# Turning the operands of a router's products, with a copy and a transpose to turn the logits back

## The reference

```
gp = softmax(ht @ rg_w + rg_b)                  # 4 groups
g_idx = argmax(gp); g_prob = gp[g_idx]
el = (ht @ re_w + re_b).reshape(T, 4, 8)[g_idx]  # 8 experts of the chosen group
top_p, top_i = top_k(softmax(el), 2)
gates = g_prob * top_p / sum(top_p)
# each token then goes through its 2 experts, of 32:
y = (silu(x @ w_gate[e]) * (x @ w_up[e])) @ w_down[e]
```

## Time and profile before

| | us |
|---|---|
| median of 3 runs | 1764.89 |
| the runs | 1764.3, 1764.89, 1767.46 |
| the profiled execution, its own time | 1770.13 |
| its span | 1768.2 |
| TensorE busy | 1724.3 (98%) |
| VectorE busy | 863.0 (49%) |
| mean granted clock of TensorE, of full | 0.993 |

### The profile page before, as it was taken

The page is one execution under the profiler, slowest core; times in us unless marked ns, Lnnn a source line. Parts: engine busy times, 40 slices in busy tenths (PEclk is TensorE's granted clock), DMA queues, the critical chain, the costliest instruction groups (busy, mean ns, idle before and its releaser), DMA issues.

```text
span 1768.2 us, 23681 instructions
## 1 busy us (share of the span) xinstructions
PE 1724.3 (98%) x9694; PEld 1136.4 (64%) x9694; DVE 863.0 (49%) x1522; ACT 485.0 (27%) x742; POOL 23.5 (1%) x31
## 2 busy tenths in 40 slices
PE   7999999999999999999999999999999999999997
PEld 6879999987789999844444444347674444444443
DVE  5678777764658777623233233232552232332323
ACT  5445444444445444310000000013431000000101
POOL 0100000000000000000000000000000000000000
PEclk9999999999999999999999999999999999999999
DMA  9535557564544646789999999997369999999995
GB/s 371 190 108 178 181 175 237 177 198 161 179 143 168 205 168 234 307 361 420 424 424 425 427 426 426 423 412 282 143 262 405 424 425 425 424 424 428 426 425 229
DMA packets 116762, 542.41 MB, mean 307 GB/s; under 512 B 5688, under 2 KB 51904, under 8 KB 88640
## 3 DMA queue, kind: packets, MB, share of 16 engines
q1 hardware_dynamic: 116240, 539.75, 77.6%
q10 hardware_dynamic: 432, 1.39, 0.2%
HBM read 540.07 MB, written 1.05 MB: 306 GB/s over the span
## 4 chain that ended last, share of the span: by engine, by line
PE 88%; DMA 4%; DVE 3%; ACT 2%; SPq 2%; POOL 1%; issue 0%; DVEq 0%; ACTq 0%; POOLq 0%
PE PS L2022 23%; PE PS L698 11%; PE PS L2052 11%; PE PS L699 11%; PE PS L700 11%; PE PS L1976 6%; DMA work<-w_up 4%; PE PS L542 2%; SPq L2136 2%; PE PS L2004 2%; PE PS L2005 1%; PE PS L2036 1%; PE PS L1520 0%; PE PS L751 0%; PE PS L1244 0%; PE PS L1830 0%
## 5 line engine op out<-in xcount | busy, mean ns | idle before, releaser
L2022 PE MATMUL PS<-ring,work 128*64 128x512 f32 x1152 | 279.7, 593 | 1.0 <-DMA ring<-w_up 1.0
L2111 DVE SCALAR_TENSOR_TENSOR work<-PS,small,work 128x512 f32<-128x512 f32 x32 | 24.0, 751 | 405.6 <-PE PS L2022 405.6
L2022 PE MATMUL PS<-work 128*64 128x512 f32 x656 | 205.2, 595 | 0.0
L2022 PEld LDWEIGHTS PS<-ring,work 128*64 128x64 f32 x1152 | 91.4, 137 | 164.7 <-issue 164.4
L2052 PE MATMUL PS<-ring,work 128*64 128x512 f32 x576 | 160.2, 598 | 1.6 <-ACT work L2077 1.6
L1976 PEld LDWEIGHTS PS<-work,hs 128*128 128x128 f32 x1024 | 121.0, 198 | 26.3 <-issue 24.3
L1976 PE MATMUL PS<-work,hs 128*128 128x128 f32 x1024 | 127.1, 284 | 1.4 <-DVE work L1959 1.4
L2022 PEld LDWEIGHTS PS<-work 128*64 128x64 f32 x656 | 66.5, 138 | 92.2 <-issue 92.2
L2052 PE MATMUL PS<-work 128*64 128x512 f32 x368 | 124.3, 598 | 0.0
L2077 ACT ACTIVATE work<-PS 128x512 f32<-128x512 f32 x32 | 19.2, 599 | 335.6 <-PE PS L2036 335.6
L1222 DVE TENSOR_TENSOR r_w_lo<-ring,r_w_hi 128x1024 fp32r<-128x1024 f32 x64 | 78.1, 1224 | 63.6 <-ACT r_w_hi L1215 62.4
(11 more groups left out here) (368 smaller groups left out, 3420.3 us busy)
## 6 DMA issues: line engine op xcount, KB each, us to landing
ring<-w_gate SPq DMA_DIRECT2D x32, 2048.0 KB, 27.2
ring<-w_down SPq DMA_DIRECT2D x32, 2048.0 KB, 25.4
ring<-w_up SPq DMA_DIRECT2D x28, 2048.0 KB, 24.5
ring<-ffn_w_up SPq DMA_DIRECT2D x22, 2048.0 KB, 8.8
work<-w_gate SPq DMA_DIRECT2D x16, 2048.0 KB, 29.3
work<-w_down SPq DMA_DIRECT2D x14, 2048.0 KB, 21.1
work<-w_up SPq DMA_DIRECT2D x14, 2048.0 KB, 21.5
ring<-ffn_w_down SPq DMA_DIRECT2D x22, 1024.0 KB, 6.2
```

The costliest lines, as they stand in the source:

```text
L2022: last = nc.tensor.matmul(PS[CAP * e:CAP * (e + 1), what, :], xg[:, c, CAP * e:CAP * (e + 1)], chunk_of(w[e], c), start=(c == 0), stop=(c ...
```

## The change

The operands of the logits' products are swapped: the 36 weight columns stand and 128 token columns of `xnT` move, so that the result is 36 x 128, logits on partitions. VectorE copies each tile to a new SBUF tile `lgT` (in the area at 2304, where `diag` and `wT` are written later). TensorE transposes each back through the identity into bank 6 + t, as 128 x 36, ahead of the fillers. The scaling instruction (now reading bank 6 + t) and all behind it stay. The counts per layer become 6 for `ro_pick` and 5 for `ro_ps`. `lgT` and all waits:

```diff
@@ build
+        lgT = area(2304, NT, P)[0:N_ROUTE, :, :]
@@ route_pe
-                    last = nc.tensor.matmul(bank(4 + t, N_ROUTE), xnT[:, c, t * P:(t + 1) * P], w[:, c, :],
+                    last = nc.tensor.matmul(bank(4 + t)[0:N_ROUTE, 0:P], w[:, c, :], xnT[:, c, t * P:(t + 1) * P],
                                             start=(c == 0), stop=(c == DC - 1))
                 last.then_inc(E("ro_ps"), 1)
+            for t in range(NT):
+                pe.wait_ge(E("ro_pick"), 6 * l + t + 1)
+                nc.tensor.transpose(bank(6 + t, N_ROUTE), lgT[:, t, :], ident[0:N_ROUTE, 0:N_ROUTE]).then_inc(E("ro_ps"), 1)
             keep_busy(FILLERS[0])
...
-                pe.wait_ge(E("ro_pick"), 4 * l + i + 1)
+                pe.wait_ge(E("ro_pick"), 6 * l + i + 3)
@@ route_act
-            act.wait_ge(E("ro_pick"), 4 * l + 3)
+            act.wait_ge(E("ro_pick"), 6 * l + 5)
...
-            act.wait_ge(E("ro_pick"), 4 * l + 4)
+            act.wait_ge(E("ro_pick"), 6 * l + 6)
@@ route_dve
             for t in range(NT):
-                dve.wait_ge(E("ro_ps"), 3 * l + t + 1)
+                dve.wait_ge(E("ro_ps"), 5 * l + t + 1)
+                v.tensor_copy(lgT[:, t, :], bank(4 + t)[0:N_ROUTE, 0:P]).then_inc(E("ro_pick"), 1)
+            for t in range(NT):
+                dve.wait_ge(E("ro_ps"), 5 * l + NT + t + 1)
                 dve.wait_ge(E("n_rstd"), NT * k + t + 1)
-                last = v.scalar_tensor_tensor(lg[:, t, :], bank(4 + t, N_ROUTE), rstd[:, t:t + 1],
+                last = v.scalar_tensor_tensor(lg[:, t, :], bank(6 + t, N_ROUTE), rstd[:, t:t + 1],
                                               G(f"route_b{l}"), ALU.mult, ALU.add)
...
-            dve.wait_ge(E("ro_pick"), 4 * l + 1)
+            dve.wait_ge(E("ro_pick"), 6 * l + 3)
...
-            dve.wait_ge(E("ro_pick"), 4 * l + 2)
+            dve.wait_ge(E("ro_pick"), 6 * l + 4)
...
-            dve.wait_ge(E("ro_ps"), 3 * l + 3)
+            dve.wait_ge(E("ro_ps"), 5 * l + 5)
@@ moe_load
-            sp.wait_ge(E("ro_ps"), 3 * l + 2)
+            sp.wait_ge(E("ro_ps"), 5 * l + 2)
```

## The result

The changed kernel takes 1767.77 us (median of 22 runs, 1764.76 to 1771.8) beside 1764.63 for the kernel before (22 runs, 1760.5 to 1770.89). The ratio is 1.0015, with a 95% interval from 1.0008 to 1.0022: 2.6 us more, between 1.4 and 3.9 (the plain medians lie 3.1 apart). The forecast was 1765.7 in 1762.8 to 1769.4, and no change by 0.2%.

The account below looks back on a forecast made before the run. TensorE was taken to bound the kernel, with VectorE's chain on the router's path. Products -0.25, copy, transpose and waits +0.65 gave +0.40 us per layer, +0.8 in all: 1765.7 us on the median, range 1762.8 to 1769.4.

Parts of the forecast that it names:

- Where the cost lies: Router's end, both layers: copy and transpose of tile 1 are on the path; a delay there counts in full.
- Products turned: Router logits: 32 records at 0.110 us instead of 0.118, a gain of 0.25 per layer; ends 0.105 and 0.118.
- rival 5: Router products: turning gains nothing, 0.118 stays; 0.65 per layer, 1766.2 us; chance 0.77 together with the forecast.
- Rival 3: Router products: weight loads not hidden, 1.1 us more per layer, 1768.0 us, still within 0.2%; chance 0.05.
- Rival 4: Router products: the narrow array runs at 0.21 us a record, +2.9 + 0.65 per layer, 1772.0 us; chance 0.02.
- Copy and transpose: Behind the router products, tile 1: copy from PSUM 0.29 us (0.19 to 0.42), transpose 0.32 with its wait (0.31 to 0.41).
- The switch ahead of transpose 0: TensorE after the last product: 0.20 us start to start instead of 0.11, covered by hand-over and copy 1 (0.33).
- Sum: Router path per layer: -0.25 + 0.04 + 0.29 + 0.04 + 0.28 = +0.40 us; ends +0.14 and +0.87.
- The time: Whole kernel: +0.8 us for both layers, 1765.7 on the median or +0.05%; same within 0.2% at chance 0.85.
- rival 1: Gather: a longer stay at the low clock, up to 2.3 us more per layer, 1770.4; slower; chance 0.10.
- The clock as the larger lever: Gather behind the router: the low clock costs 5.96 - 3.77 = 2.2 us per layer, which the change doesn't touch.
- Rival 2: Gather: no low clock, since 128 columns move per product; -2.2 us per layer, 1761.3; faster; chance 0.06.

Follow-up runs that it names:

- after_wide: The changed kernel with 108 weight columns standing instead of 36, the rows above 36 not read; 1.0017 [1.0004, 1.0031] of the kernel before.
- the second sample: The changed kernel timed again, unchanged, beside the kernel before; ratio 1.0004 [0.9993, 1.0015], mean of 11 runs 1767.59 beside 1766.06 us.
- before_pause: The kernel before with two waited-for SBUF copies (0.5 us) ahead of VectorE's scaling of tile 1; 1.001 [0.9999, 1.0022] of the kernel before.

## Why the prediction was right, and which terms were off

*Where the cost lies.* Right. The copy of tile 1 and its transpose are on the path in both layers, and copy 0 and transpose 0 lie beside other work. Nothing later is seen to absorb it: the time rose by 1.4 us at least in the first set.

*Products turned.* The mis-sized term: forecast 0.110 per record and a gain of 0.25, measured 3.70 / 32 = 0.116 and a gain of 0.07. The two-record sample of L591 was too small to tell 0.110 from 0.116; over 32 records the pace of 128 columns moving is nearly that of the 128-column loads before. It lies within the ends, near the upper one, and rival 5 (nothing gained) came closest. Rival 3 (loads not hidden) fell by after_wide, and with it the rule of the Trainium skill (TensorE: Matmul & The Clock Gate, Part 3) that loads and products of the same rows don't overlap: 60 ns more of load cost 2 ns. Rival 4 (0.21) fell too.

*Copy and transpose.* 0.29 and 0.32 forecast, 0.28 to 0.29 and 0.04 + 0.26 measured. The switch ahead of transpose 0 takes 0.20 from start to start, as in the earlier trace rows, and is covered by copy 1 as forecast. It takes 0.20 with 108 columns standing too, so the narrow stationary operand, from which the forecast saw the array switched, isn't its cause; whether it is a drain no run tells.

*Sum.* 0.40 per layer forecast, 0.54 measured, within the ends of 0.14 and 0.87. The products' pace added 0.18 to the forecast, and the turn back took 0.04 less (0.61 against 0.65).

*The time.* 0.8 forecast, 1.1 on the path, 2.6 by the ratio, with 1.4 as the lower end; the second sample gave 0.0004, or 0.7, with 1.5 between the means. In both sets the mean granted clock is no lower than before (0.9954 over 22 runs and 0.9956 over 11, against 0.9950, 0.9955 and 0.9955 for the kernel before), so rival 1 in its plain form, a longer stay at the low clock, isn't shown. The runs can also be compared at the same granted clock. At 0.994, 0.995 and 0.996 the kernel before takes 1767.2, 1765.8 and 1764.9 on average (14, 15 and 17 of 108 runs), the changed kernel 1769.5, 1768.1 and 1767.3 (5, 7 and 14 of 33). That is 2.3 to 2.4 more; with one straight line in the clock fitted to the runs of all kernels it is 2.0, with a standard error of some 0.25. So the clock doesn't account for what lies beyond the 1.1 of the path, and about 1 us has no place in any profile here. The comparison mixes sets, since the clocks of the kernel before were not kept in the first one. Read in the same way before_pause lies 1.5 above the kernel before (standard error 0.4), so a price of the longer wait alone, with no turned product, is possible; it isn't shown. That the time came out inside the forecast's range, with more than twice the 0.8 that was forecast, owes something to the width of that range, most of which is the scatter of the runs.

*The clock as the larger lever.* Right as to its size: a gather takes 3.84 to 6.70 us. What decides between them is open. More fillers behind the second call went with 3.84 in all twelve gathers, but ten fillers had it in six of sixteen. Rival 2 (no low clock, because 128 columns move) isn't borne out: the changed kernel's four gathers took 4.21, 5.36, 5.27 and 5.37, and with the same 128 moving columns after_wide has 6.70 and 5.28.

## What to carry to other kernels

Swapping the operands of small float32 products trades a wide load for a wide stream at nearly the same pace, 0.118 against 0.116 here; here it paid only with a second step, two column groups side by side (0.062 a record). A turn back through a copy and a transpose cost 0.62 us here, where the result is waited for, so count it before the swap. In a kernel where the clock moves a stage by 2 us and the code's length a branch by 4, a change of 1 us is read from its stage in the chain, not from one run.

## What was not expected of the hardware

- The same gather, behind the same instructions, took 5.96, 5.97, 6.08 and 3.84 us in the two profiles of the kernel before. Where the low clock falls changes from layer to layer and from run to run; in three stages it fell in the 24 fillers instead, which then took 4.6 us and not 3.12.
- Four products more in TensorE's stream brought a wait of 4.05 us behind a branch some 440 us later, in each of the three kernels with 4 or 8 more. The runs with four more took 3.5 to 5.5 us longer, and in each of the three the transfer of instructions that precedes that place elsewhere fell inside the wait.
- The mean time of the kernel before falls with the granted clock, from 1771 at 0.992 to 1764 at 0.997 (32 runs, a correlation of -0.86): the spread of its runs is mostly the clock.
